# Retention with both scan directions stacked on the partitions, and the scores and inner values in front of the scan

## The reference

```python
def step(s, qkv):
    qc, kc, vc = qkv
    scores = einsum('bhid,bhjd->bhij', qc, kc) * intra
    o = (einsum('bhij,bhjv->bhiv', scores, vc)
         + einsum('bhid,bhdv->bhiv', qc * q_dec[..., None], s))
    s = s * c_dec[..., None] + einsum('bhjd,bhjv->bhdv', kc * k_dec[..., None], vc)
    return s, o
# o_f from (q, k, v) forwards, o_b the same on flipped sequences; o = o_f + flip(o_b)
# the latent scans start from the context's final state; in the last layer
# the context gives only k and v
```

## Time and profile before

| | |
|---|---|
| median of three runs | 3023.5 us |
| the profiled execution | 3025.06 us, its span 3023.1 us |
| PE busy | 2748.1 us, 91% |
| weight loads of PE | 2235.7 us, 74% |
| DVE busy | 2116.0 us, 70% |
| POOL busy | 999.4 us, 33% |
| ACT busy | 702.2 us, 23% |
| chain that ended last | PE 78%, DVE 10%, POOL 4% |

### The profile page before, as it was taken

One profiled execution on the slowest core, in us unless ns is written; L12 is line 12 of the kernel. 1 busy time (PEld: TensorE's weight loads), 2 busy tenths in 40 slices (PEclk: granted clock), 3 DMA queues, 4 the chain that ended last, 5 costly groups with the idle time before them and its releaser, 6 DMA issues.

```text
span 3023.1 us, 37020 instructions
## 1 busy us (share of the span) xinstructions
PE 2748.1 (91%) x13212; PEld 2235.7 (74%) x13212; DVE 2116.0 (70%) x3515; ACT 702.2 (23%) x1400; POOL 999.4 (33%) x941
## 2 busy tenths in 40 slices
PE   5999898488999999999999599998598999999995
PEld 3777776377788888888887487786476888888884
DVE  4778785667667667667768798763756667766777
ACT  3222334323210110110111323334323111111111
POOL 1244354456111111111112544453663122222225
PEclk9999999799999999999999799999798999999998
DMA  8222222441122222222220211111522111111111
GB/s 238 87 76 69 86 83 76 127 140 36 38 82 70 70 83 70 70 77 76 70 43 21 97 41 60 58 48 33 154 70 70 42 49 48 49 49 47 50 45 59
DMA packets 245115, 215.64 MB, mean 71 GB/s; under 512 B 58336, under 2 KB 201232, under 8 KB 245008
## 3 DMA queue, kind: packets, MB, share of 16 engines
q10 hardware_dynamic: 139776, 117.46, 13.0%
q1 hardware_dynamic: 105232, 96.81, 10.6%
HBM read 191.60 MB, written 22.63 MB: 71 GB/s over the span
## 4 chain that ended last, share of the span: by engine, by line
PE 78%; DVE 10%; POOL 4%; DMA 2%; issue 2%; ACT 2%; SPq 1%; ACTq 0%; POOLq 0%; DVEq 0%
PE bank L523 14%; PE bank L525 13%; PE bank L524 13%; PE bank L993 9%; PE bank L995 9%; PE bank L994 9%; PE bank L867 2%; PE bank L868 2%; PE bank L869 2%; PE bank L603 1%; PE bank L927 1%; PE bank L926 1%; DVE x_hl L1435 1%; PE bank L910 1%; DVE x_hl L1433 1%
## 5 line engine op out<-in xcount | busy, mean ns | idle before, releaser
L1398 POOL TENSOR_TENSOR w_lo<-raw,w_hi 128x1024 fp32r<-128x1024 f32 x120 | 288.6, 2406 | 1196.1 <-ACT w_hi L1246 1196.1
L993 PE MATMUL bank<-x_hl,w_hi 128*128 128x512 f32 (+1 forms) x1280 | 475.6, 372 | 0.0
L994 PE MATMUL bank<-x_hl,w_hi 128*128 128x512 f32 (+1 forms) x1280 | 473.4, 370 | 0.0
L995 PE MATMUL bank<-x_hl,w_lo 128*128 128x512 f32 (+1 forms) x1280 | 473.1, 370 | 0.0
L523 PE MATMUL bank<-w_hi,h_hi 128*128 128x512 f32 x1152 | 450.9, 391 | 9.9 <-DVE work L1668 8.0
L524 PE MATMUL bank<-w_lo,h_hi 128*128 128x512 f32 x1152 | 448.9, 390 | 0.0
L525 PE MATMUL bank<-w_hi,h_lo 128*128 128x512 f32 x1152 | 448.8, 390 | 0.0
L1645 DVE TENSOR_TENSOR work<-work 128x512 f32<-128x512 f32 (+1 forms) x160 | 146.5, 915 | 430.5 <-ACT work L1237 430.5
L1571 DVE SCALAR_TENSOR_TENSOR bank<-work,bank 128x512 f32<-128x512 f32 (+1 forms) x580 | 407.2, 702 | 18.9
L1668 DVE TENSOR_TENSOR work<-work,bank 128x512 f32<-128x512 f32 x576 | 396.1, 688 | 19.6
L1666 DVE TENSOR_TENSOR bank<-bank,work 128x512 f32<-128x512 f32 x576 | 398.8, 692 | 0.2
(11 more groups left out here) (142 smaller groups left out, 4362.9 us busy)
## 6 DMA issues: line engine op xcount, KB each, us to landing
raw<-in_w_ff ACTq DMA_DIRECT2D x128, 512.0 KB
work<-in_w_ada SPq DMA_DIRECT2D x48, 512.0 KB
raw<-in_w_in ACTq DMA_DIRECT2D x64, 256.0 KB
plain_words<-in_w_ada ACTq DMA_DIRECT2D x64, 256.0 KB
raw<-in_w_in ACTq DMA_DIRECT2D x16, 512.0 KB
plain_words<-in_w_ada SPq DMA_DIRECT2D x16, 512.0 KB, 12.1
raw<-in_w_out ACTq DMA_DIRECT2D x16, 512.0 KB
gate_rows<-work SPq DMA_DIRECT2D x72, 64.0 KB, 1.6
```

The costliest lines, as they stand in the source:

```text
L993: nc.tensor.matmul(o, slot(mlp_slot(l, f), 0)[:, wc], x_hi[:, k, cols], start=k == 0, stop=False)
L994: nc.tensor.matmul(o, slot(mlp_slot(l, f), 0)[:, wc], x_lo[:, k, cols], start=False, stop=False)
L995: mm = nc.tensor.matmul(o, slot(mlp_slot(l, f), 1)[:, wc], x_hi[:, k, cols], start=False, stop=k == KT - 1)
L1398: nc.gpsimd.tensor_tensor(slot(mlp_slot(l, sl), 1), raw[:, un % 2, :], slot(mlp_slot(l, sl), 0).bitcast(F32), ALU.subtract).then_inc(w_rea ...
```

## The change

- The two directions now lie on the two halves of the partitions (`HALVES`), in tiles that are stored in the order of the scan. The state of a pair is one 128 x 128 block per tile; forwards above, backwards below.
- POOL scales k instead of v (`k_sc`), and also q (into the raw tile), each for both directions. PE transposes four pieces in place of two, and the state update is two 64-column products.
- A row's scores follow its `post` by one step, and a new action `attend` (scores times v) follows by one more, in front of the scan; ACT keeps the result (`o_intra`).
- Behind the scan a row is ACT's two half copies of the state, one pair of 64-column products, and one addition on DVE. A pair's first values stand in the step behind its scan. In the tail these products go round three PSUM banks.
- v is kept in a ring of four tiles, k in two. The held-back `evac` is gone; a `post` is held back instead, at most one a step.
- The convolution stores each run as it ends, from two buffers.

```diff
-        now = ready[:1] if ready and ready[0] in scored else []
...
+        scores_now, to_score = to_score, []
+        attend_now, to_attend = to_attend, []
+        tail = n > len(steps) + 1
+        for p, t in ready[:1]:
+            plan.append(("values", p, t, tail, scores_now[0] if scores_now and not tail else None))
+            valued.add(ready.pop(0))
         while evacs and evacs[0] <= n:
             kind, p, t = steps[evacs[0]]
-            if kind == "Q" and p and t in tiles and (p - 1, t) not in valued:
-                break
...
-        while posts and k < 2 and evac_at.get(posts[0], n) < n:
+        post_now = None
+        if posts and evac_at.get(posts[0], n) < n:
             kind, p, t = steps[posts[0]]
-            plan.append(("post", posts.pop(0)))
-            k += 1
+            if not p or t not in tiles or (p - 1, t) in valued:
+                post_now = posts.pop(0)
+        for p, t in attend_now:
+            plan.append(("attend", p, t, post_now))
+        if post_now is not None:
+            kind, p, t = steps[post_now]
+            plan.append(("post", post_now, attend_now[0] if attend_now else None))
+            if t in tiles:
+                to_score.append((p, t))
             if t == NT - 1:
                 plan.append(("scan", p))
                 assert not p or all((p - 1, u) in valued for u in tiles)
                 ready += [(p, u) for u in tiles]
+        for p, t in scores_now:
+            plan.append(("scores", p, t))
+            to_attend.append((p, t))
```

PE's part of `post` and `values`, and ACT's of `post`:

```diff
+                            pe.wait_ge(S["qsc_done"], s0["qsc_done"] + row_of(l, p, t) + 1)
+                            for i, piece in enumerate((src, qk_raw[:, q % 2, :])):
+                                for h in range(2):
+                                    nc.tensor.transpose(ps_tr[:, (2 * i + h) * P:(2 * i + h + 1) * P], piece[:, h * P:(h + 1) * P], ident)
...
-                        nc.tensor.matmul(ps_u[:, 0:2 * P], src[:, P:2 * P], v_dec, start=True, stop=True).then_inc(S["u_done"], 1)
...
+                            mm = nc.tensor.matmul(ps_u[:, h * DK:(h + 1) * DK], k_sc[:, h * P:(h + 1) * P], v_sb[:, q % 4, h * DK:(h + 1) * DK], start=True, stop=True)
...
-                        nc.tensor.matmul(ps_o[:, P:3 * P], qk_t[:, t, 0, :], s_diag[:, r % 2, :], start=True, stop=True).then_inc(S["val_done"], 1)
...
+                            mm = nc.tensor.matmul(ps_value(l, r, tail)[:, h * DK:(h + 1) * DK], qd_t[:, t, h * P:(h + 1) * P], s_both[:, r % 2, h * DK:(h + 1) * DK], start=True, stop=True)
...
-                            nc.scalar.activation(qk_t[:, t, :, :], ps_tr.rearrange("p (a b) -> p a b", b=P), ACT.Copy).then_inc(S["post_evac"], 1)
...
+                            nc.scalar.activation(k_t[:, r % 2, :], ps_tr[:, P:2 * P], ACT.Copy)
+                            for h in range(2):
+                                r64 = slice(h * DK, (h + 1) * DK)
+                                nc.scalar.activation(q_diag[r64, r % 2, h * P:(h + 1) * P], ps_tr[r64, 0:P], ACT.Copy)
+                            nc.scalar.activation(qd_t[:, t, :], ps_tr[:, 2 * P:], ACT.Copy).then_inc(S["post_evac"], 1)
```

DVE's part of `values`:

```diff
-                        nc.vector.tensor_tensor(inter.rearrange("p (a e) -> p a e", e=DK), ps_o[:, P:3 * P].rearrange("p (a e) -> p a e", e=DK),
-                                                q_dec[:, 2 * p:2 * p + 2, :].rearrange("p a b -> p (a b)").unsqueeze(2).to_broadcast([P, 4, DK]), ALU.mult).then_inc(S["comb_a"], 1)
...
+                        nc.vector.tensor_tensor(o_out[:, r % 2, :], ps_value(l, r, tail), o_intra[:, t, :], ALU.add).then_inc(S["comb_done"], 1)
```

More of the change, by code:

```diff
@@ L123, in mix_in_plan @@
     finished, stored, pause, consumed = [], [], 2, False
-    while n < len(steps) or posts or len(valued) < PAIRS * len(tiles) or pieces or finished or stored:
+    while n < len(steps) or posts or to_score or to_attend or len(valued) < PAIRS * len(tiles) or pieces or finished or stored:
         if n < len(steps):
@@ L254, in layer_counts @@
     pairs.update({name: 8 * n for name in "o_in g_in cv_in res_in".split()})
+    pairs["cv_st"] = 32 * runs
     return counts, pairs
@@ L913, in _ @@
                         r = row_of(l, p, t)
-                        pe.wait_ge(S["qd_done"], s0["qd_done"] + r + 1)
+                        pe.wait_ge(S["post_evac"], s0["post_evac"] + r + 1)
                         if r:
                             pe.wait_ge(S["prob_done"], s0["prob_done"] + r)
-                        nc.tensor.matmul(ps_sc[:, 0:2 * P], qk_t[:, t, 1, :], q_diag[:, r % 2, :], start=True, stop=True).then_inc(S["score_done"], 1)
+                        earlier = [b for b in plan[:plan.index(a)] if b[0] == "values" and b[4] != (p, t) and not b[3]]
@@ new lines, in _ @@
+                        if earlier:
+                            pe.wait_ge(S["comb_done"], s0["comb_done"] + len(earlier))
+                        nc.tensor.matmul(ps_sc[:, 0:2 * P], k_t[:, r % 2, :], q_diag[:, r % 2, :], start=True, stop=True).then_inc(S["score_done"], 1)
+                    elif a[0] == "attend":
+                        _, p, t, _ = a
+                        r, q = row_of(l, p, t), p * NT + t
+                        pe.wait_ge(S["prob_done"], s0["prob_done"] + r + 1)
+                        if r:
+                            pe.wait_ge(S["att_evac"], s0["att_evac"] + r)
+                        posted = sum(1 for b in plan[:plan.index(a)] if b[0] == "post")
+                        if posted:
+                            pe.wait_ge(S["u_evac"], s0["u_evac"] + posted)
+                        for h in range(2):
+                            mm = nc.tensor.matmul(ps_att[:, h * DK:(h + 1) * DK], probs[:, r % 2, h * P:(h + 1) * P], v_sb[:, q % 4, h * DK:(h + 1) * DK], start=True, stop=True)
+                        mm.then_inc(S["att_done"], 1)
@@ L918, in _ @@
                     elif a[0] == "values":
[L919 removed]
+                        _, p, t, tail, _ = a
                         r = row_of(l, p, t)
[L921 removed]
                         pe.wait_ge(S["sd_done"], s0["sd_done"] + r + 1)
[L923 to L924 removed]
+                        if tail:
+                            pe.wait_ge(S["evac_q"], s0["evac_q"] + n * PAIRS)
+                            pe.wait_ge(S["comb_done"], s0["comb_done"] + r - 2)
+                        else:
+                            if r:
+                                pe.wait_ge(S["comb_done"], s0["comb_done"] + r)
+                            scored = sum(1 for b in plan[:plan.index(a)] if b[0] == "scores")
+                            if scored:
+                                pe.wait_ge(S["prob_done"], s0["prob_done"] + scored)
@@ L928, in _ @@
+                        mm.then_inc(S["val_done"], 1)
                     elif a[0] == "ada":
@@ L1124, in _ @@
                         nc.scalar.activation(k_dec_raw[:, :, 1], decay[:, 1, :], ACT.Exp, scale=expo[:, 3:4])
-                        for h in range(2):
-                            rows64 = slice(h * DK, (h + 1) * DK)
-                            last = nc.scalar.activation(c_dec[rows64, :, :], decay[rows64, :, h::2], ACT.Exp, scale=-float(P))
+                        for d, (half, _) in enumerate(HALVES):
+                            last = nc.scalar.activation(c_dec[half, :], decay[half, d, :], ACT.Exp, scale=-float(P))
                         last.then_inc(S["dec_op"], 1)
@@ L1187, in _ @@
                             act.wait_ge(S["val_done"], s0["val_done"] + r - 1)
-                        for h in range(2):
-                            r64 = slice(h * DK, (h + 1) * DK)
-                            last = nc.scalar.activation(s_diag[r64, r % 2, h * P:(h + 1) * P].rearrange("p (a b) -> p a b", b=DK), state[r64, t, :, :], ACT.Copy)
+                        for half, order in HALVES:
+                            last = nc.scalar.activation(s_both[half, r % 2, :], state[half, order.index(t), :], ACT.Copy)
                         last.then_inc(S["sd_done"], 1)
```

180 lines of the change are left out of this document (89 added, 91 removed).

## The result

| | before | after |
|---|---|---|
| median | 3022.3 us (four runs, 3018.6 to 3023.6) | 3070.0 us (four runs, 3066.5 to 3073.7) |
| ratio | | 1.0160, interval 1.0148 to 1.0173 |
| profiled span, mean granted clock | 3023.1 us, 0.953 | 3068.9 us, 0.943 |

The account below looks back on a forecast made before the run. PE was taken to bound the kernel, the question being whether it is kept fed. Terms 5.8 + 4 + 22.8 + 4 - 9.6 - 7.1 summed to +19.9 us, forecasting a median of 3043 us, range 3017 to 3060.

Parts of the forecast that it names:

- Term 1: PE's small operations in the mixing of both layers: +0.08 us in each of 72 rows, +5.8 us.
- Term 2: DVE and ACT work of a row in the mixing: hidden beside PE's step of 7.4 us, 0.
- term 4: First row behind each of six scans: PE waits for the scan's end and the state copy, +22.8 us.
- Term 3: POOL's scaled queries: hidden except behind the last tile of a pair, six places, +4 us.
- rival of contention that goes: At the scans: POOL contention goes, order stays, scan takes 3.3 us, six waits sum to about 6; 3025 us, chance 0.14.
- Term 5: Lower PE clock behind the waits at the six scans: +4 us, bounds 0 and 10.
- Terms 6 and 7: Tails of layers 0 and 1: shorter by 9.6 us (bounds 4 and 13) and 7.1 us (bounds 3 and 10).
- Term 8: The convolution's stores in runs with two buffers, on SP: 0, at most 1 us.
- longer rows bite everywhere: Rival, all rows: added DVE and ACT waits cost 0.4 us more each; 3080 us, 3058 with a quarter; chance 0.08.

Follow-up runs that it names:

- experiments 5 and 6: Scores product of the last pair done twice: in the changed kernel 3077.9 us, in the kernel before 3022.75 us, respectively.
- experiments 1 and 11: Changed kernel, pairs 0 and 1's first values two steps behind the scan: 3063.8 us; with pairs 0-2's scan also placed behind its step's scores: 3046.55 us.
- experiment 10: Changed kernel with the weight copies of a step placed behind its values, nothing else: 3014.6 us, ratio 0.9973 to the kernel before.
- experiment 2: Changed kernel with the two transposes of the scaled q done twice in every row: 3080.5 us, ratio 1.0192 to the kernel before.

## Why the prediction was wrong

The direction was right, the size not: +19.9 us forecast, +46 measured, outside the range. By its own terms:

- **Term 1, PE's work (+5.8), failed**, and it is the larger part of the miss. Measured +27.9. The row costs +0.21, not +0.08: x72 is 15. I took the inner values at 0.39, the four transposes at 0.44 and the scores at 0.43; behind one another the inner values and the transposes take 0.44 and 0.45, and the scores, now the last operation in front of the projection, take 0.05 more than the update that stood there. That is 0.11 of the 0.13. And I counted rows, not where they stand: 14 rows of scores and of their products with v moved from the tails, where PE has room, in front of the end of the last projection, about 12 us (experiments 5 and 6 show for the scores that such an operation is paid for after and free before). The two make 27 of the 27.9.
- **Term 2, DVE beside PE (0), held in this kernel**, in the steady state. Behind a scan it was only hidden under the wait of term 4: it appears with the cover (experiments 1 and 11).
- **Term 3, POOL (+4), didn't show.** PE waits over 1 us for POOL at three of the six last posts only, 6.9 us together after and 7.9 before (at the earlier trace rows and its two likes).
- **Term 4, the exposed scan (+22.8), stood**: 20.3 at six places, released by ACT's state copy, as worked out. Its mechanism had a part that I named and did not price: I wrote that the weight copy that releases the split stands right behind ACT's row, and so kept the split in the scan. Right for this kernel; but it means that the wait hangs on the order of ACT's queue, and experiment 10 halves it without touching the scan. My rival of contention that goes is what that kernel does.
- **Term 5, the clock (+4), failed by a factor of four**: +15.3. I priced the loss at one wait by 1.7 us and let most waits go free. Behind the six waits at the scans it was 0.50 to 0.64 for 4 us, so 1.4 to 2 us lost at each. With the waits at the scans and at the loads taken away (experiment 10) the clock costs 13.1 us in the regions, less than the 22.8 before: most of it goes with the waits. Not all: experiment 2 lost 8 us less to the clock at the same idle time.
- **Terms 6 and 7, the tails (-9.6 and -7.1), stood within their bounds**: -7.8 and -4.7. In layer 1 the scan starts 12.0 us behind the start of the last projection product (2133.17) where it was 9.8 (2082.86), so 2.2 us later, as forecast (2.4); but from its end to the last store go 13.0 us, not 11. In layer 0 it is 20.3, not 19.
- **Term 8, the stores (0), stood**: the middle sections agree within 1.5 us.

With the idle time of the regions at +16.5 where terms 3 and 4 said 26.8, the misses are +22.1 (term 1), +11.3 (5), -10.3 (3 and 4), +4.2 (tails) and -1.5 (middle): 26, which is the 45.8 us of the spans less the 19.9 forecast. The rival "longer rows bite everywhere" would have given the time (3058 to 3080), but not for its reason: no wait per row is to be seen, only PE's own work.

What remains argued and not shown: how the 55 us of experiment 10 split between the scans and the load steps once the clock is counted, since one edit removes both; and why the same idle time costs more of the clock in one execution than in another.

## What to carry to other kernels

Price an operation that is moved by the place it goes to: the same product was free in a tail in which PE waits and cost its full length in front of the last projection. When an engine waits for a producer, write down every operation that hangs on it (here state copy and masking) and what stands ahead of each in its queue, for covering one of them only moves the wait. And before a restructuring, look at what a queue holds up with a long copy: moving one action in the list gave 19 us in the old kernel and 55 in the new, more than the 46 that the restructuring cost.

## What the runs showed of the hardware

- The scan is 18 operations on two SBUF operands: 5.76 us with a 2.39 us split of POOL beside it, 3.61 in the same kernel and place once the split comes behind it; the difference is 2.15 us. The Trainium skill (SBUF — State Buffer, Who interferes with whom) says that one of the two is held for the length of the other; experiment 10 agrees with it, to within 0.24 us. With four shorter operations of POOL beside it (2.3 us, layer 0, pair 2 of the same run) the scan took 4.99 us, 1.4 more, so less than their sum.
- A pair of fp32 products of 64 columns takes 0.39 to 0.44 us to the next start, one product of 256 columns 0.43 to 0.49: half the columns in all save a fifth of the time at most.
- Behind the six waits of 2.53 to 4.23 us at the scans of the kernel after, the granted clock of the next 4 us was 0.50 to 0.64. Behind waits of 2.46 and 2.92 us in the kernel before (ended at 226.96 and 357.11) it stayed at 1.00, so the length of the one wait doesn't settle it. Experiment 10 removed 31 us of idle and gave 25 us of clock back, nearly as much again.
